# A decoder step's last combine, spread over VectorE, ScalarE and GpSimd

## The reference, cut to what matters

```python
def rms_norm(x, g):
    y = xf * lax.rsqrt(jnp.mean(xf * xf, axis=-1, keepdims=True) + EPS)
    return (y * g).astype(x.dtype)
...
        yp = yp + hier_moe(rms_norm(yp, norm2[l]), *moe_w)   # 32 experts, two per token
        ys = ys + hier_moe(rms_norm(ys, norm2[l]), *moe_w)
    yp = rms_norm(yp, norm_f)
    ys = rms_norm(ys, norm_f)
```

## Time and profile before

| | us |
|---|---|
| median of 3 runs | 666.19 (664.97 to 666.68) |
| the profiled execution | 667.25 |
| its span, first to last instruction | 665.5 |
| TensorE busy | 579.6 (87%) |
| VectorE busy | 317.1 (48%) |
| ScalarE busy | 226.5 (34%) |
| GpSimd busy | 71.8 (11%) |

### The profile page before, as it was taken

The page is one execution under the profiler, slowest core; times in us unless marked ns, Lnnn a source line. Parts: engine busy times, 40 slices in busy tenths (PEclk is TensorE's granted clock), DMA queues, the critical chain, the costliest instruction groups (busy, mean ns, idle before and its releaser), DMA issues.

```text
span 665.5 us, 8773 instructions
## 1 busy us (share of the span) xinstructions
PE 579.6 (87%) x2808; PEld 355.4 (53%) x2808; DVE 317.1 (48%) x653; ACT 226.5 (34%) x390; POOL 71.8 (11%) x136
## 2 busy tenths in 40 slices
PE   3899899999999999999899888999999779988800
PEld 3676596877778777777478643433333223323200
DVE  5834667767767667677565853210110000100038
ACT  5423425375573755646253211111111111111122
POOL 1200070000000000004000011122121111210000
PEclk9899999999999999999898969999999999988955
DMA  8411324732212222221692589999999999999764
GB/s 313 149 72 65 126 80 183 331 103 71 88 65 93 85 71 95 102 63 63 220 393 98 206 328 420 420 420 418 421 420 421 421 419 421 418 421 420 299 266 164
DMA packets 33159, 160.60 MB, mean 241 GB/s; under 512 B 6288, under 2 KB 6672, under 8 KB 20464
## 3 DMA queue, kind: packets, MB, share of 16 engines
q1 hardware_dynamic: 27520, 149.52, 56.7%
q0 software_dynamic: 5472, 10.63, 4.3%
q10 hardware_dynamic: 144, 0.15, 0.1%
HBM read 155.01 MB, written 14.17 MB: 254 GB/s over the span
## 4 chain that ended last, share of the span: by engine, by line
PE 59%; SPq 18%; DVE 10%; DMA 7%; ACT 3%; issue 2%; DVEq 0%; ACTq 0%; POOLq 0%; POOL 0%
SPq L528 17%; PE ps L1408 13%; PE ps L1409 12%; PE ps L1410 12%; PE ps L1755 5%; DMA wslot<-in_wmoe 5%; PE ps L1776 4%; PE ps L1526 2%; PE ps L1558 2%; DVE x L1389 2%; PE ps L1612 1%; PE ps L1510 1%; PE ps L1417 1%; PE ps L1549 1%; DVE yf L1381 1%
## 5 line engine op out<-in xcount | busy, mean ns | idle before, releaser
L1755 PE MATMUL ps<-wslot,xgT 128*64 128x512 f32 x528 | 125.4, 608 | 13.1 <-DMA wslot<-in_wmoe 11.6
L688 ACT ACTIVATE wh<-raw 128x1024 fp32r<-128x1024 f32 x56 | 59.1, 1057 | 165.5 <-PE ps L1410 146.9
L1408 PE MATMUL ps<-xh,wh 128*128 128x512 f32 x256 | 102.5, 400 | 0.0
L1410 PE MATMUL ps<-xl,wh 128*128 128x512 f32 x256 | 99.9, 390 | 0.0
L1409 PE MATMUL ps<-xh,wl 128*128 128x512 f32 x256 | 99.9, 390 | 0.0
L1755 PEld LDWEIGHTS ps<-wslot,xgT 128*64 128x64 f32 x528 | 41.4, 140 | 92.9 <-issue 91.2
L888 DVE TENSOR_TENSOR wl<-raw,wh 128x1024 fp32r<-128x1024 f32 x53 | 66.6, 1256 | 48.9 <-ACT wh L688 47.9
L1776 PE MATMUL ps<-wslot,hT 128*64 128x512 f32 x264 | 62.1, 598 | 8.9 <-ACT hT L853 7.1
L1354 DVE SCALAR_TENSOR_TENSOR hm<-ps,rt,hs 128x256 f32<-128x256 f32 x12 | 5.8, 484 | 124.8 <-ACT hs L851 124.8
L1408 PEld LDWEIGHTS ps<-xh,wh 128*128 128x128 f32 x256 | 48.1, 188 | 16.1 <-issue 6.7
L1410 PEld LDWEIGHTS ps<-xl,wh 128*128 128x128 f32 x256 | 48.0, 188 | 10.6
(11 more groups left out here) (299 smaller groups left out, 779.6 us busy)
## 6 DMA issues: line engine op xcount, KB each, us to landing
wslot<-in_wmoe SPq DMA_DIRECT2D x99, 1024.0 KB, 27.1
raw<-in_wmix SPq DMA_DIRECT2D x56, 512.0 KB, 3.9
gy<-ytok SPq DMA_DIRECT2D x8, 512.0 KB, 6.6
xt<-in_x SPq DMA_DIRECT2D x4, 512.0 KB, 6.9
x<-in_x SPq DMA_DIRECT2D x4, 512.0 KB, 4.5
xnd<-x SPq DMA_DIRECT2D x4, 512.0 KB, 5.6
out_y<-yf SPq DMA_DIRECT2D x4, 512.0 KB, 2.6
gw<-in_wgate POOLq DMA_DIRECT2D x8, 128.0 KB, 2.3
```

Source lines behind the costliest of these rows:

```text
L688: a.activation(WH[hslot], raw[:, slot, :, :].rearrange("p k c -> p (k c)"), ACT.Copy).then_inc(hi_ready, 1)
L1408: pe.matmul(out, sh, mh_, start=start, stop=False)
L1410: return pe.matmul(out, sh, ml_, start=False, stop=stop)
L1755: l = pe.matmul(ps[CAP * s:CAP * s + CAP, 2, :], xgT[:, c, CAP * s:CAP * s + CAP], wslot[q][s][:, c * 512:(c + 1) * 512], start=c == 0, st ...
```

## The change

- The last two scatters take their indices straight from the table `idx`; the copy to `coly` and the wait for it are left out there.
- SyncE reads the sample rows (tile 4) first, then tiles 0 to 3. It stores in the order 0, 1, 4, 2, 3.
- The combine of the sample rows leaves VectorE: ScalarE multiplies each slot's rows by their gates, GpSimd adds them to `x1`.
- The final products of tiles 0 and 4 leave VectorE: ScalarE multiplies the row by the inverse root, GpSimd multiplies by `norm_f`.
- Division by 1024 and epsilon go into ScalarE's Sqrt (scale, and a column `eps` as bias), so `mean_square` is gone. A Sqrt on one column stands ahead of the last stretch on ScalarE.
- VectorE keeps eight combines, five reciprocals (`inverse`) and three final products.

The diff, without the declarations of the semaphores:

```diff
+LENGTHS = (0, NT, 1, 2, 3)
...
@@ -559,12 +566,12 @@
 
             e.wait_ge(y_out, nx * 16 + 16 * PAIRS)
             e.sem_inc(held, 1)
-            for t in range(TILES):
+            for t in (NT, *range(NT)):
                 r = rowsof(t)
                 for s in range(2):
                     e.dma_start(gy[0:r, s, t, :], ytok[s * TA + t * P:s * TA + t * P + r, :]).then_inc(back_in[t], 16)
-            for t in range(TILES):
-                e.wait_ge(fin_ready, t + 1)
+            for t, ready, count in ((0, pool_final, 1), (1, fin_ready, 1), (NT, pool_final, 2), (2, fin_ready, 2), (3, fin_ready, 3)):
+                e.wait_ge(ready, count)
                 e.dma_start(y_tiles[t], yf[0:rowsof(t), t, :]).then_inc(done_out, 16)
             e.wait_ge(v_stored, 32)
             e.wait_ge(done_out, 16 * (TILES + 1))
@@ -637,6 +644,12 @@
                 g.sem_inc(held, 1)
                 gather_at(colg[:, 0:1])
 
+            def scatter_at(offsets):
+
+                g.indirect_dma_start(
+                    out=ytok, out_offset=bass.IndirectOffsetOnAxis(ap=offsets, axis=0),
+                    in_=yo[:, :], in_offset=None, bounds_check=2 * TA - 1, oob_is_err=False).then_inc(y_out, 16)
+
             def scatter(table, column, count):
 
                 g.wait_ge(yo_sb, FIRST + count)
@@ -644,9 +657,7 @@
                 g.tensor_copy(coly[:], table[:, 1, column]).then_inc(coly_copied, 1)
                 g.wait_ge(coly_copied, count)
                 g.sem_inc(held, 1)
-                g.indirect_dma_start(
-                    out=ytok, out_offset=bass.IndirectOffsetOnAxis(ap=coly[:, 0:1], axis=0),
-                    in_=yo[:, :], in_offset=None, bounds_check=2 * TA - 1, oob_is_err=False).then_inc(y_out, 16)
+                scatter_at(coly[:, 0:1])
 
             g.wait_ge(xn_stored, 16 * TILES)
             g.wait_ge(xg_zero, 1)
@@ -671,7 +682,24 @@
                 gather(idxx, bass.ds(m + 2, 1), m + (HEAD + 2))
                 scatter(idxx, bass.ds(m, 1), m + (HEAD + 1))
             for n in (2, 1):
-                scatter(idxx, bass.ds(nx + (TAIL - n), 1), nx + (PAIRS - n + 1))
+                g.wait_ge(yo_sb, FIRST + nx + (PAIRS - n + 1))
+                g.sem_inc(held, 1)
+                scatter_at(idx[:, 1, PAIRS - n:PAIRS - n + 1])
+
+            def times_weight(t):
+
+                r = rowsof(t)
+                g.tensor_tensor(yf[0:r, t, :], yf[0:r, t, :], nf[0:r, :], ALU.mult).then_inc(pool_final, 1)
+
+            g.wait_ge(const_in, NCONST)
+            for s in range(2):
+                g.wait_ge(gated_rows, s + 1)
+                g.tensor_tensor(x1[0:S, NT, :], gy[0:S, s, NT, :], x1[0:S, NT, :], ALU.add).then_inc(sample_comb, 1)
+                g.wait_ge(sample_comb, s + 1)
+            g.wait_ge(scaled, 1)
+            times_weight(0)
+            g.wait_ge(scaled, 2)
+            times_weight(NT)
 
 
         @block.scalar
@@ -865,15 +893,39 @@
             nx = a.value_load(nxi[0:1, 0:1], min_val=0, max_val=EXTRA)
             with a.Fori(0, nx + TAIL) as m:
                 expert_pass(m + HEAD, rtx[:, bass.ds(m, 1)], True)
+            a.activation(warm[:], ones[:, 0:1], ACT.Sqrt)
             a.dma_start(st, so[:]).then_inc(done_out, 16)
 
-            for t in range(TILES):
+            def length(t):
+
                 r = rowsof(t)
-                a.wait_ge(comb, 2 * t + 2)
-                a.wait_ge(n2_sq, 2 * TILES + t)
+                if t == NT:
+                    a.wait_ge(sample_comb, 2)
+                else:
+                    a.wait_ge(comb, 2 * t + 2)
+                a.wait_ge(n2_sq, 2 * TILES + LENGTHS.index(t))
                 a.activation(junk3[0:r, :], x1[0:r, t, :], ACT.Square, accum_out=ss[0:r, t:t + 1]).then_inc(n2_sq, 1)
-                a.wait_ge(fin_ms, t + 1)
-                a.activation(rstd[0:r, t:t + 1], ss[0:r, t:t + 1], ACT.Sqrt).then_inc(fin_sq, 1)
+                a.wait_ge(n2_sq, 2 * TILES + LENGTHS.index(t) + 1)
+                a.activation(rstd[0:r, t:t + 1], ss[0:r, t:t + 1], ACT.Sqrt, scale=1.0 / D, bias=eps[0:r, :]).then_inc(fin_sq, 1)
+
+            def scale(t):
+
+                r = rowsof(t)
+                a.wait_ge(fin_rs, LENGTHS.index(t) + 1)
+                a.activation(yf[0:r, t, :], x1[0:r, t, :], ACT.Copy, scale=rstd[0:r, t:t + 1]).then_inc(scaled, 1)
+
+            a.wait_ge(gates_ready, 1)
+            a.wait_ge(back_in[NT], 32)
+            for s in range(2):
+                a.activation(gy[0:S, s, NT, :], gy[0:S, s, NT, :], ACT.Copy,
+                             scale=gate[0:S, s, POS[NT]:POS[NT] + 1]).then_inc(gated_rows, 1)
+            length(0)
+            length(NT)
+            length(1)
+            scale(0)
+            scale(NT)
+            length(2)
+            length(3)
 
 
         @block.vector
@@ -974,6 +1026,7 @@
                 own.then(d.tensor_copy(hi_, tv))
                 own.then(d.tensor_tensor(tokc[:, 1].rearrange("p y s t -> p (y s t)"), tv, hi_, ALU.subtract))
                 own.then(d.tensor_tensor(wrt[:], wrt[:], ch[:, :, C_G2:C_G2 + 1].broadcast_to([P, KT, NL]), ALU.mult))
+                d.memset(eps[:], EPS)
                 d.memset(ssa[:], float(D) / 2).then_inc(so_ready, 1)
 
 
@@ -1286,6 +1339,7 @@
             own.then(d.reciprocal(r1[:, 6, :], r1[:, 6, :]))
             own.then(d.tensor_tensor(gate[:, 0, :], r1[:, 6, :], r1[:, 5, :], ALU.mult))
             own.then(d.tensor_tensor(gate[:, 1, :], gate[:, 0, :], r1[:, 3, :], ALU.mult))
+            d.sem_inc(gates_ready, 1)
 
             nck = MAXCHUNK - 1
 
@@ -1369,34 +1423,36 @@
                 rows_T(m + (HEAD + 1))
             gated(nx + (PAIRS - 1), rtx[:, bass.ds(nx + (TAIL - 1), 1)])
 
-            def mean_square(t):
+            def inverse(t):
+
                 r = rowsof(t)
-                d.wait_ge(n2_sq, 2 * TILES + 1 + t)
-                d.tensor_scalar(ss[0:r, t:t + 1], ss[0:r, t:t + 1], 1.0 / D, EPS, ALU.mult, ALU.add).then_inc(fin_ms, 1)
+                d.wait_ge(fin_sq, LENGTHS.index(t) + 1)
+                d.reciprocal(rstd[0:r, t:t + 1], rstd[0:r, t:t + 1]).then_inc(fin_rs, 1)
 
             def final(t):
-                r = rowsof(t)
-                d.wait_ge(fin_sq, t + 1)
-                own.then(d.reciprocal(rstd[0:r, t:t + 1], rstd[0:r, t:t + 1]))
-                d.scalar_tensor_tensor(out=yf[0:r, t, :], in0=x1[0:r, t, :], scalar=rstd[0:r, t:t + 1], in1=nf[0:r, :],
+
+                d.wait_ge(fin_rs, LENGTHS.index(t) + 1)
+                d.scalar_tensor_tensor(out=yf[:, t, :], in0=x1[:, t, :], scalar=rstd[:, t:t + 1], in1=nf[:],
                                        op0=ALU.mult, op1=ALU.mult).then_inc(fin_ready, 1)
 
             d.wait_ge(const_in, NCONST)
-            for t in range(TILES):
-                r = rowsof(t)
+            for t in range(NT):
                 d.wait_ge(back_in[t], 32)
                 for s in range(2):
-                    d.scalar_tensor_tensor(out=x1[0:r, t, :], in0=gy[0:r, s, t, :], scalar=gate[0:r, s, POS[t]:POS[t] + 1],
-                                           in1=x1[0:r, t, :], op0=ALU.mult, op1=ALU.add).then_inc(comb, 1)
+                    d.scalar_tensor_tensor(out=x1[:, t, :], in0=gy[:, s, t, :], scalar=gate[:, s, POS[t]:POS[t] + 1],
+                                           in1=x1[:, t, :], op0=ALU.mult, op1=ALU.add).then_inc(comb, 1)
                     if s == 0:
                         d.wait_ge(comb, 2 * t + 1)
-                if t >= 1:
-                    mean_square(t - 1)
-                if t >= 2:
-                    final(t - 2)
-            final(NT - 1)
-            mean_square(NT)
-            final(NT)
+                if t == 1:
+                    inverse(0)
+                if t == 2:
+                    inverse(NT)
+                    inverse(1)
+            final(1)
+            inverse(2)
+            final(2)
+            inverse(3)
+            final(3)
 
 
         @block.tensor
```

More of the change, by code:

```diff
@@ L253, in build @@
     turn = small("turn", [P, 4])
+    eps = small("eps", [P, 1])
     WH, WL = (wh[:, 0, :], wh[:, 1, :], wh2[:]), (wl[:, 0, :], wl[:, 1, :], wl2[:])
@@ L365, in build @@
         comb = sem("comb")
-        fin_ms = sem("fin_ms")
+        fin_rs = sem("fin_rs")
+        scaled = sem("scaled")
+        pool_final = sem("pool_final")
+        sample_comb = sem("sample_comb")
+        gates_ready = sem("gates_ready")
+        gated_rows = sem("gated_rows")
         fin_sq = sem("fin_sq")
```

## The result

The changed kernel takes 669.8 us, median of 14 runs, beside 666.35 of the kernel before, also 14 runs. One run of the changed kernel took 3277.4 us, for a reason that nothing here shows, and is left out of the ratio; the other 13 lie between 667.1 and 670.9. The ratio is 1.0045 with a 95% interval of 1.0032 to 1.0058: the change makes the kernel 3.0 us slower (2.1 to 3.9), less than half a per cent. Forecast were 2.8.

A forecast was written before the change was run, and what follows sets the result against it. TensorE and the weight queue bound the span; the change touches only the serial, VectorE-bound tail. VectorE sheds 5.3 us, GpSimd turns add 7.4, ending at 665.2 not 663.1; the store adds 0.7: 666.2 + 2.8 = 669.0 us, range 663.8 to 671.6.

The forecast's parts named there:

- Turns of the engines: In the tail, four GpSimd operations alternate with VectorE's: three cost 2.1 us each, one 1.1, 7.4 in all.
- The scatter: Behind the last eviction, leaving out the index copy saves 0.3 us; bounds 0 and 1.04.
- Samples read first: On the SP queue, two 128 KB reads ahead delay tile 0 by 0.6 us; upper bound two issues, 0.9.
- VectorE's own work: In the tail, eight combines and three products, 14.1 us, plus about 0.5 for reciprocals and gaps.
- The last store: At the end, tile 3's 512 KB instead of the samples' 128 KB lands in 2.6 us, not 1.9: 0.7 more.
- ScalarE: In the tail, about 12 us of added work in a window of 20, ready before VectorE asks: costs nothing.
- Rival one: In the tail, VectorE and GpSimd overlap, VectorE ends at 657.8, time 661.6 us; chance 0.15.
- Rival two: In the tail, VectorE keeps its place and GpSimd waits until it stands still; time 671.5 us; chance 0.1.
- Rival three: In the tail, turns but cheaper: samples sooner, a product in a wait, or full scatter saving; 666.2 us; chance 0.15.

The follow-up runs named there:

- e1: The changed kernel without GpSimd's two final products, rows of tile 0 and samples stored as ScalarE scaled them; ratio 0.9983 to the kernel before.
- e2: The changed kernel with all four GpSimd operations cut to 64 of 1024 columns, every wait kept; ratio 0.9956 to the kernel before.
- e5: The kernel before with only the last two scatters taking indices straight from the table; ratio 1.0007 to the kernel before.
- e6: The kernel before with only the order of reads changed, sample rows first; ratio 1.0026 to the kernel before.
- e8: e7 with its last two products and stores exchanged, the samples' 128 KB before tile 3's 512 KB; ratio 0.9993 to the kernel before.
- e3: The kernel before plus four two-input GpSimd multiplications of 128x1024 that nobody waits for; ratio 1.0105 to the kernel before.
- e9: e3 with VectorE's ten combines reading one operand from PSUM instead of the rows read back; ratio 0.9992 to the kernel before.
- e7: The changed kernel without elementwise work on GpSimd: VectorE does the sample combines and all five final products, samples' last; ratio 0.9974 to the kernel before.
- e4: The kernel before plus four one-input GpSimd multiplications of 128x1024 that nobody waits for; ratio 1.0049 to the kernel before.

## Why the prediction was right

The direction and the mechanism were right, and so was the size (2.8 forecast, 3.0 measured), but that it came so close is in part luck. Term by term, misses of up to 1.2 us cancelled:

- **Turns of the engines**, forecast 7.4, measured 6.2 in the trace. The three full turns cost 1.9, 2.0 and 2.0 where I had 2.1. The first cost 0.3 where I had 1.1: the sample rows landed 2.2 and 2.4 after their issues, not 3.0, so the first add had begun earlier. e1 and e2 show that it is these operations and their length: without two of them VectorE ends 3.7 sooner behind the eviction, with all four short 5.3, and 4.2 and 6.2 if the later landing of tile 0 in these profiles is taken out.
- **The scatter**, forecast 0.3 (bounds 0 and 1.04), measured 0.44 here and 0.46 in e5.
- **Samples read first**, forecast 0.6, upper bound 0.9; measured 0.9 here and 1.2 in e6. The time on the wire was the wrong measure: tile 0's second read is issued 1.30 behind the first of all reads instead of 0.37, and then takes 4.6 as before. Two more issues on SP, 2 × 0.42 plus gaps, are the whole 0.9. I had called this the bound and not taken it.
- **VectorE's own work**: without the holds it runs 14.4 from the first combine to the last product (20.6 − 6.2), where I had 14.6.
- **The last store**, forecast 0.7, measured 1.4. e8 gives 0.6 to the size. The rest goes, as far as the landings tell, to stores that crowd at the end. I had put the other stores at nothing with the sentence that those of tile 0 and the samples hold nothing up, and had not asked about those of tiles 1 and 2.
- **ScalarE** costs nothing, as forecast: in the changed kernel's chain VectorE never waits for it. Its terms add up to 11.2 us, not "about 12"; nothing hangs on it.

Together VectorE ends 0.9 later behind the eviction instead of 2.1, and the store adds 1.4 instead of 0.7: 2.2 in the tail, 0.6 under the forecast, which the interval of the timing (2.1 to 3.9) just holds. The other 0.8 of the measured 3.0 no term of the prediction explains.

Rival one, that the engines overlap, is refuted for these operations by e2 and e3; e9 shows when it would have held. Rival two, that GpSimd is starved, is refuted for two-input operations: the longest took 3.3. Rival three came true in its first part, an add that is nearly through when tile 0 arrives, but that was worth 0.8 and not a whole turn.

## What to carry to other kernels

Before you give elementwise work to GpSimd to relieve VectorE, look what VectorE does in the same microseconds: if it reads two tensors from SBUF (a copy was held as well, see below), a two-input GpSimd operation costs VectorE nearly as much time as it runs (1.7 to 2.0 us for 1024 columns, where VectorE needs 1.28 to do the work itself). Look instead for time in which VectorE waits: here the sample rows fitted before tile 0's landing once they were read first, and the kernel that used this (e7) was the faster one. And when the last engine's work is reordered, price the last store by its size, and look at what is issued just before it.

## What the hardware showed beyond that

- VectorE with one operand in PSUM and one in SBUF was not held at all: ten combines at 1.27 to 1.285 beside four GpSimd products (e9), against up to 3.02 with both in SBUF (e3). "GPSIMD Engine Reference" of the Trainium skill, Key points, names two SBUF inputs, or a two-port performance mode, as the condition on VectorE's side; this case agrees for the two inputs.
- Two SBUF inputs are not the only form that is held. In the kernel before, a copy of eight columns (L1068, 0.17 otherwise) began at 314.49, inside GpSimd's last subtraction, and lasted until 316.48, when that had ended (316.45). A copy of one column just ahead of it took its usual 0.15:

```profile
L1068 DVE COPY so<-xc x8: 173/174/1992, 121.4 to 314.5; 128x8 f32 x7, 128x8 f32<-128x8 f32 x1
L1067 DVE COPY so<-xc x8: 154/154/156, 121.1 to 314.3; 128x1 f32 x7, 128x1 f32<-128x1 f32 x1
```

- A two-input GpSimd operation of 1024 columns runs as long on 32 rows (2.34 in the changed kernel) as on 128 (2.40), and 1.89 when both inputs are the same tile.
- A one-input GpSimd operation of 1024 columns cost VectorE 0.7 us and itself lasted 2.8 to 3.9 beside a busy VectorE (e4).
